# Router logits with the weights stationary in four 32-column groups, and the softmax one step later

## The reference

```
x = x + gt_m * rms_norm(mix, g_post_mix)
h = rms_norm(x, g_pre_ffn) * (1.0 + sc_f) + sh_f
aff = softmax(h @ w_router)              # 16 experts
top_v, top_i = top_k(aff.T, 2 * n // 16) # each expert picks its tokens: 32 of 256, 128 of 1024
```

## Time and profile before

| | us |
|---|---|
| median of 3 runs | 2684.17 |
| the profiled execution | 2684.22 |
| its span in the profile | 2682.4 |
| PE busy | 2538.7 (95%) |
| DVE busy | 1661.7 (62%) |
| ACT busy | 1330.4 (50%) |
| DMA moved | 345.06 MB, mean 129 GB/s |

### The profile page before, as it was taken

One profiled execution on the slowest core, in us unless ns is written; L12 is line 12 of the kernel. 1 busy time (PEld: TensorE's weight loads), 2 busy tenths in 40 slices (PEclk: granted clock), 3 DMA queues, 4 the chain that ended last, 5 costly groups with the idle time before them and its releaser, 6 DMA issues.

```text
span 2682.4 us, 37869 instructions
## 1 busy us (share of the span) xinstructions
PE 2538.7 (95%) x15199; PEld 1936.3 (72%) x15199; DVE 1661.7 (62%) x2553; ACT 1330.4 (50%) x2262; POOL 285.8 (11%) x287
## 2 busy tenths in 40 slices
PE   7999699999999999999999999996899999999994
PEld 3574499999788587676767887883677777777773
DVE  2654678886333435757576435557677767777775
ACT  3542467776423324444444333442666767666663
POOL 1441101100000001010101000000010101111012
PEclk8999899999999999999999999997899999999997
DMA  9320000000211100101002201436698898989886
GB/s 322 130 91 16 0 1 1 1 1 1 74 37 71 62 16 24 32 24 33 14 27 83 79 32 47 188 111 223 216 308 309 273 315 288 312 282 311 303 272 213
DMA packets 176608, 345.06 MB, mean 129 GB/s; under 512 B 9338, under 2 KB 37580, under 8 KB 176434
## 3 DMA queue, kind: packets, MB, share of 16 engines
q1 hardware_dynamic: 166396, 314.09, 33.0%
q0 software_dynamic: 9472, 28.32, 4.1%
q10 hardware_dynamic: 566, 0.24, 0.0%
HBM read 304.35 MB, written 38.27 MB: 128 GB/s over the span
## 4 chain that ended last, share of the span: by engine, by line
PE 62%; issue 23%; DMA 8%; DVE 4%; ACT 2%; POOL 1%; POOLq 0%; SPq 0%; DVEq 0%; ACTq 0%
PE ps L1100 16%; PE ps L1449 7%; PE ps L851 6%; DMA ffn_scratch<-WK 6%; PE ps L823 5%; PE ps L1409 5%; PE ps L228 4%; PE ps L1991 4%; PE ps L1512 2%; PE ps L1495 1%; PE ps L1423 1%; PE ps L2534 1%; PE ps L2017 1%; PE ps L1472 1%; PE ps L1393 1%
## 5 line engine op out<-in xcount | busy, mean ns | idle before, releaser
L2613 ACT ACTIVATE RWr<-R 128x1024 fp32r<-128x1024 f32 x384 | 377.7, 1054 | 72.1 <-PE ps L2534 69.4
L2708 DVE TENSOR_TENSOR W_low<-R,RWr 128x1024 fp32r<-128x1024 f32 x256 | 301.4, 1220 | 84.5 <-ACT RWr L2613 82.5
L2534 PE MATMUL ps<-RWr,R1r 128*128 128x512 f32 x1024 | 329.6, 396 | 6.0 <-DVE R1r L2696 4.2
L1100 PE MATMUL ps<-W_high,tile_high 128*128 128x512 f32 x640 | 250.9, 392 | 7.8 <-DVE W_low L1178 7.3
L1100 PE MATMUL ps<-W_low,tile_high 128*128 128x512 f32 x640 | 250.5, 391 | 0.0
L1100 PE MATMUL ps<-W_high,tile_low 128*128 128x512 f32 x640 | 250.4, 391 | 0.0
L2534 PEld LDWEIGHTS ps<-RWr,R1r 128*128 128x128 f32 x1024 | 192.9, 188 | 58.3 <-issue 14.2
L1170 DVE TENSOR_TENSOR tile_low<-R,tile_high 128x1024 fp32r<-128x1024 f32 x80 | 97.9, 1224 | 156.8 <-ACT tile_high L1126 156.6
L1449 PE MATMUL ps<-R3r 128*128 128x512 f32 (+1 forms) x640 | 188.4, 371 | 2.9 <-issue 2.9
L2708 DVE TENSOR_TENSOR tile_high<-R,RWr 128x1024 fp32r<-128x1024 f32 x128 | 150.8, 1220 | 29.9 <-ACT RWr L2613 29.6
L2534 PE MATMUL ps<-RWr,R3r 128*128 128x512 f32 x512 | 166.7, 397 | 0.0
(11 more groups left out here) (373 smaller groups left out, 5068.7 us busy)
## 6 DMA issues: line engine op xcount, KB each, us to landing
R<-in_w_dram SPq DMA_DIRECT2D x96, 2048.0 KB, 13.3
RW<-in_w_in_dram SPq DMA_DIRECT2D x11, 1024.0 KB, 5.4
R<-in_w_mod_dram SPq DMA_DIRECT2D x5, 2048.0 KB, 13.6
RW<-in_w_in_dram SPq DMA_DIRECT2D x5, 2048.0 KB, 8.3
RW<-in_w_mod_dram SPq DMA_DIRECT2D x4, 2048.0 KB, 11.7
WK<-in_w_mod_dram SPq DMA_DIRECT2D x3, 2048.0 KB, 8.0
mix_scratch<-R SPq DMA_DIRECT2D x10, 512.0 KB, 2.6
R<-mix_scratch SPq DMA_DIRECT2D x10, 512.0 KB, 6.9
```

What stands on the lines that cost most here:

```text
L1100: i = pe.matmul(bank(m % 4), Tsplit[a][:, m % 2, k, :], Wsplit[b][:, k, :], start=(k == 0 and n == 0), stop=(k == KD - 1 and n == 2))
L2534: m = pe.matmul(bank(bank_of(e, i, j)), stat[a][:, k, :], w[b][:, k % 2, :], start=(k == 0 and z == 0), stop=(k == KD - 1 and z == 2))
L2613: act.activation(ring_high[n % RING], pair_raw[i][j][:, 2 * q:2 * q + 2, :], ACT.Copy).then_inc(S("weights_high"), 1)
L2708: dve.tensor_tensor(ring_low[n % RING], pair_raw[i][j][:, 2 * q:2 * q + 2, :], ring_high[n % RING].bitcast(F32), ALU.subtract).then_inc(S( ...
```

## The change

The router's weights become the stationary operand, in groups of 32 columns (16 of weights and 16 of zeros), and the turned tile moves: product k goes to column group k % 4, two products per group, so that PSUM partitions 32c to 32c+31 hold the c-th partial sum of the logits, experts on the partitions. ACT copies the 128x128 block to SBUF (`keep_logit_sums`), and one more product with the copy stationary and the 0/1 matrix `sel_e` moving adds the four groups and turns the result in one (`logits`), into columns 128 to 143 of bank 6. The softmax reads those.

In the loops `logits(t-2)` stands behind `project(t, 1)` and ahead of `turn(t-1)`; `soft` goes from tile t-2 to tile t-3 and `turn_aff` and `keep_aff` from t-3 to t-4; `keep_logit_sums(t-2)` stands behind `soft(t-3)` on ACT. The route waits for `router_exp` of the tile before, in place of `aff_made`. The rounds of `best_eight` move from t = 5 to 8 to t = 6 to 9. The loops have NT + 4 steps.

```diff
--- before.py
+++ after.py
@@ -33,6 +33,7 @@
 NE = 16
 CAP_CTX, CAP_LAT = 2 * N_CTX // NE, 2 * N_LAT // NE
 CAP = CAP_CTX + CAP_LAT
+GROUP = 32
 EPS = 1e-6
 SCALE = float(HD) ** -0.5
 GSCALE = float(DK) ** -0.5
@@ -117,7 +118,8 @@
         st = sb("st", [P, 64])
         mhalf = sb("mhalf", [P, 16])
         w_lr = sb("w_lr", [P, KD, 2 * RANK])
-        wr = sb("wr", [P, KD * NE + P - NE])
+        wr = sb("wr", [P, KD, GROUP])
+        sel_e = sb("sel_e", [P, NE])
         with nc.sbuf_tensor("WK", [P, WORK_N], F32) as WK:
             pass
 
@@ -318,7 +320,7 @@
                 *((vv[:, 0:4, g * VW:g * VW + HD], cache_v[0, 0, g].rearrange("(b p) d -> p b d", p=P)) for g in range(HKV)),
                 (keep[:, :], k_keep),
                 (w_lr[:, :, :], win[:, C_LR:C_LR + 2 * RANK].rearrange("(k p) n -> p k n", p=P)),
-                (wr[:, 0:KD * NE].rearrange("p (k n) -> p k n", k=KD), w_router[0].rearrange("(k p) n -> p k n", p=P)),
+                (wr[:, :, 0:NE], w_router[0].rearrange("(k p) n -> p k n", p=P)),
             ):
                 sp.dma_start(dst, src, allow_slow_non_contiguous=True).then_inc(S("cache_landed"), 16)
                 n += 16
@@ -552,7 +554,7 @@
         def pool_front(pool, ch):
             pool.memset(cS4[:, :, :], 0.0).then_inc(S("cond_ready"), 1)
             ch(pool.memset(mhalf[:, :], -0.5))
-            ch(pool.memset(wr[:, KD * NE:], 0.0))
+            ch(pool.memset(wr[:, :, NE:], 0.0))
             ch(pool.memset(vv[:, :, HD::VW], 1.0))
 
             def load(t):
@@ -611,6 +613,7 @@
             ch(dve.memset(varq, 1.0))
             dve.wait_ge(S("bias_landed"), 16 * 8)
             ch(dve.tensor_reduce(sel, ident[:, :].rearrange("p (c m) -> p m c", c=4)[:, 0:2, :], AX, ALU.add))
+            ch(dve.tensor_reduce(sel_e[:, :], ident[:, :].rearrange("p (c m) -> p m c", c=4)[:, 0:NE, :], AX, ALU.add))
             dve.wait_ge(S("mod_columns"), 1)
             dve.wait_ge(S("cond_ready"), 2)
             ch(dve.tensor_copy(gv[:, :, :].rearrange("p n k -> p (n k)"), vcols[:, 56:80]))
@@ -1924,6 +1927,7 @@
 
         colb = R2[:, N_TOK:N_TOK + BLK].rearrange("p (k n) -> p k n", k=4)
         aff = R2[:, N_TOK + BLK:N_TOK + BLK + 2 * NE].rearrange("p (a n) -> p a n", a=2)
+        logit_sums = [R2[:, N_TOK + n * P:N_TOK + (n + 1) * P] for n in range(2)]
         G2b = [RW[:, j * D:(j + 1) * D] for j in range(2)]
         so = st[:, 0:24]
 
@@ -2009,13 +2013,18 @@
                 pe.wait_ge(S("h2_kept_act"), t + 1)
                 pe.wait_ge(S("h2_kept_dve"), t + 1)
                 if t >= 1:
-                    pe.wait_ge(S("aff_made"), t)
+                    pe.wait_ge(S("router_exp"), t)
                 else:
                     pe.wait_ge(S("rows_kept"), 4)
                 for k in range(KD):
 
-                    m = pe.matmul(bank(6, P), h2T[t % 2][:, k, :], wr[:, k * NE:k * NE + P], start=(k == 0), stop=(k == KD - 1))
+                    c_ = k % 4
+                    m = pe.matmul(ps[c_ * GROUP:(c_ + 1) * GROUP, 6 * BANK:6 * BANK + P], wr[:, k, :], h2T[t % 2][:, k, :], start=(k < 4), stop=(k >= 4))
                 m.then_inc(S("routed"), 1)
+
+            def logits(t):
+                pe.wait_ge(S("logit_sums_kept"), t + 1)
+                pe.matmul(ps[:, 6 * BANK + P:6 * BANK + P + NE], logit_sums[t % 2], sel_e[:, :], start=True, stop=True).then_inc(S("logits_turned"), 1)
 
             def turn_aff(t):
                 pe.wait_ge(S("aff_made"), t + 1)
@@ -2026,21 +2035,23 @@
 
             mix_turn(0)
             pe_bcast(pe, 0, 6)
-            for t in range(NT + 3):
+            for t in range(NT + 4):
                 if t < NT:
                     project(t, 0)
                 if t < 2:
                     pe_bcast(pe, 1 + 2 * t, 6)
                 if 0 <= t - 2 < NT:
                     route(t - 2)
-                if 0 <= t - 3 < NT:
-                    turn_aff(t - 3)
+                if 0 <= t - 4 < NT:
+                    turn_aff(t - 4)
                 if t + 1 < NT:
                     mix_turn(t + 1)
                 if t < NT:
                     project(t, 1)
                 if t == 0:
                     pe_bcast(pe, 2, 6)
+                if 0 <= t - 2 < NT:
+                    logits(t - 2)
                 if 0 <= t - 1 < NT:
                     turn(t - 1)
             end(pe, "pe")
@@ -2081,8 +2092,14 @@
 
             def soft(t):
                 act.wait_ge(S("router_max"), t + 1)
-                act.activation(aff[:, t % 2, :], bank(6, NE), ACT.Exp, bias=so[:, 8:9], accum_out=so[:, 9:10]).then_inc(S("router_exp"), 1)
+                act.activation(aff[:, t % 2, :], ps[:, 6 * BANK + P:6 * BANK + P + NE], ACT.Exp, bias=so[:, 8:9], accum_out=so[:, 9:10]).then_inc(S("router_exp"), 1)
                 act.wait_ge(S("router_exp"), t + 1)
+
+            def keep_logit_sums(t):
+                act.wait_ge(S("routed"), t + 1)
+                if t >= 2:
+                    act.wait_ge(S("logits_turned"), t - 1)
+                act.activation(logit_sums[t % 2], bank(6, P), ACT.Copy).then_inc(S("logit_sums_kept"), 1)
 
             def keep_aff(t):
                 act.wait_ge(S("aff_turned"), t + 1)
@@ -2097,11 +2114,13 @@
                     weights_high(cb, k)
                     if (cb, k) == (0, 1):
                         tile_high(0)
-            for t in range(NT + 3):
+            for t in range(NT + 4):
+                if 0 <= t - 3 < NT:
+                    soft(t - 3)
                 if 0 <= t - 2 < NT:
-                    soft(t - 2)
-                if 0 <= t - 3 < NT:
-                    keep_aff(t - 3)
+                    keep_logit_sums(t - 2)
+                if 0 <= t - 4 < NT:
+                    keep_aff(t - 4)
                 if t + 1 < NT:
                     tile_high(t + 1)
                 if t < NT:
@@ -2185,8 +2204,8 @@
                 dve.sem_inc(S("h2_kept_dve"), 1)
 
             def soft(t):
-                dve.wait_ge(S("routed"), t + 1)
-                ch(dve.tensor_reduce(so[:, 10:11], bank(6, NE), AX, ALU.max))
+                dve.wait_ge(S("logits_turned"), t + 1)
+                ch(dve.tensor_reduce(so[:, 10:11], ps[:, 6 * BANK + P:6 * BANK + P + NE], AX, ALU.max))
                 if t >= 2:
                     dve.wait_ge(S("aff_turned"), t - 1)
                 dve.tensor_scalar(so[:, 8:9], so[:, 10:11], -1.0, None, ALU.mult).then_inc(S("router_max"), 1)
@@ -2203,11 +2222,11 @@
                         tile_low(0)
                     if k == 3:
                         keep_row(cb)
-            for t in range(NT + 2):
+            for t in range(NT + 4):
                 if t == 1:
                     keep_row(3)
-                if 0 <= t - 2 < NT:
-                    soft(t - 2)
+                if 0 <= t - 3 < NT:
+                    soft(t - 3)
                 if t + 1 < NT:
                     tile_low(t + 1)
                 if t == 0:
@@ -2217,10 +2236,10 @@
                 if t < NT:
                     residual(t)
                     normal(t)
-                if 0 <= t - (T_CTX + 3) < CAP_CTX // 8:
+                if 0 <= t - (T_CTX + 4) < CAP_CTX // 8:
 
                     dve.wait_ge(S("aff_kept"), T_CTX)
-                    best_eight(dve, ch, 0, t - (T_CTX + 3))
+                    best_eight(dve, ch, 0, t - (T_CTX + 4))
             end(dve, "dve")
```

## The result

The changed kernel takes 2735.07 us (median of 4 runs, 2732.46 to 2737.3) against 2684.34 us for the kernel before beside it: 1.0185 times as long, 95% interval 1.0172 to 1.0197, so 50.7 us slower. Forecast were 2727.9 us, or 43.7 us slower, with a range of 2711.5 to 2745.5. The profiled execution took 2737.3 us, the longest of the four; its span is 2735.5.

A forecast was written before the change was run, and what follows sets the result against it. PE was taken as the bound, with a new closed loop through the delayed softmax. Terms 23.0 + 4.4 + 15.4 - 1.4 + 2.3 = +43.7 us on 2684.22 gave 2727.9 us, range 2711.5 to 2745.5.

The forecast's parts named there:

- The wait as the mechanism: PE's route, steps 3 to 9: it waits for the delayed exponential, due 10.74 us after the turn; +23.0 us over seven steps.
- The loop's length: Steady step from 0/1 product through exponential and route to the next turn: 18.22 us against 14.94, +3.28 each.
- rival 2: PE's route: the column groups don't run together and it stays at 1.88 us; 2745 us in all, chance 0.06.
- Entering the groups: PE, start of a burst of grouped products: costs about 0.08 us.
- Best eight: VectorE rounds behind the norm delay the exponential: 1.48 us each, three in steps 7 to 9, +4.4 us.
- The clock: PE behind each idle gap runs at a lowered clock: 2.2 us lost each, seven times, +15.4 us.
- Rival 1: PE behind the gaps: the clock holds over gaps of this length; +28.3 us, 2712.5 us in all, chance 0.10.
- rival 3: PE behind the gaps: clock never recovers before the turn, 7.2 us per gap instead of 2.2; 2763 us, chance 0.05.
- Step 2 and the tail: Step 2 routes tile 0 with a shorter route and no softmax wait, -1.4 us; the stage's last tiles, +2.3 us.
- Sum for the stage: Stage that projects the mix and routes: all terms together +43.7 us, passed through to the kernel's end.
- The memset and the load of the router's weights only change shape: nothing: Router's weights set-up: no cost, as no engine waits there.
- Rival 4: Exponential is there when PE reaches the route: 1.18 us saved in each of 8 steps; about 2677 us, chance 0.05.

The follow-up runs named there:

- the one wait alone: Kernel before, with one added wait: the route of tile t also waits for the norm of tile t+1; 2718.21 us, 1.0125 times the kernel before.
- the filled gap: Changed kernel with 17 or 23 spare 512-column products, which nobody reads, ahead of the route's wait; 2723.36 us.
- the last kernel: Changed kernel with softmax in its old step, no buffer moved, best-eight rounds behind the next mix tile's split; 2674.88 us, 0.9967 times the kernel before.
- The kernel with the buffers in place: Changed kernel with the router's weights in their old 240 words and the 0/1 matrix behind the last buffer; 2728.26 us, 1.0162 times the kernel before.

## Why the prediction was right, point by point

- The wait as the mechanism, its place and its seven times: shown. PE idles in front of the route in seven steps of the loop, released by the exponential; the one wait alone gives 38 us in the stage of the old kernel; and the same softmax with the route behind it costs next to nothing.
- The loop's length, 18.22 us: 18.15 measured with the clock held (the filled gap). In it: the turn to the exponential 10.76 for 10.74; the route 0.46 for 0.45 (1761.47 to 1761.93 in the last kernel), so the groups do run together and the bound of 1.88 is out (rival 2); the 0/1 product 0.14 for 0.25. Entering the groups costs 0.1 us in a full queue: in the last kernel the route starts 0.32 us behind the projection before it, where those stand 0.22 to 0.23 apart. That the affinities' turn changes the mode already, as the prediction says, was not tested.
- Best eight, 1.48 each on the loop: 19.63 against 18.15.
- A term that the sum lacked: the table load of ScalarE, 1.28 us in the first of the seven steps (21.68 with the half clock, 19.22 with the gap filled). The errors elsewhere in the loop hide it: 147.4 us for the seven steps forecast, 148.2 measured.
- The clock, 2.2 a gap and 15.4 in all: 15.8. The 2.2 was a choice just above the 2.1 and 1.7 of the earlier trace rows; that it came out to a tenth is in part luck, as the step with a round of best eight lost 2.8 (22.47 against 19.63). Rival 1 (the clock holds) is out, rival 3 (it stays down until the turn) too: it is back some 5 us behind the gap's end. The Trainium skill's advice against idle gaps between matmuls (TensorE: Matmul & The Clock Gate, Why this matters for your kernels) held, at 2.26 us a gap.
- Step 2 and the tail, -1.4 and +2.3: -0.9 and +2.8. In the tail it is 3.9 more in front of the last turn, for 3.7, and 1.1 less behind it, for 1.4. The last route took 0.46 us and not 0.9, as the clock was at 1.00 there again.
- Sum for the stage: 43.7 forecast, 45.1 measured in the profiled run (43.2, 2.8 and -0.9). The kernel with the buffers in place is 43.9 us slower as a whole.
- "The memset and the load of the router's weights only change shape: nothing": here the prediction failed, by 7 us. The weights' buffer grew by 16 words and got a neighbour of 16, so each buffer allocated behind it lay 128 bytes further on, and the experts' products ran 1% slower for 740 us. This is the distance between the forecast and the result: 2727.9 was forecast, and the kernel with the buffers in place took 2728.26. The stated range held it, though nothing in that range was meant for this; the prediction's own narrower range for its forecast ended at 2736.
- Rival 4 (faster) is out as a forecast, but its price was nearly right: where the route doesn't wait, the step is 13.86 us, a gain of 1.08 for the 1.18 reckoned.

## What to carry to other kernels

When a step of a software pipeline is delayed by one turn, ask of each wait that names it where its signal now falls in the waiting engine's step. Here a softmax that came 4.4 us too late for its waiter in the same step closed a loop over all engines and cost 27 us, and the idle gaps that it opened cost 16 more by the clock. And a buffer that changes size moves all behind it: keep the addresses (put the new buffer last) or measure the move alone, before a change of 1% is judged.

## What the runs showed that had not been expected

- Buffers moved by 64 or 128 bytes per partition made 738.8 us of matmuls take 746.0 to 747.6 (products 0.230 apart instead of 0.227, clock 1.00), among them products whose own operands had not moved, as those from RWr and R1r. A move of 256 bytes gave 739.0. The stages before were not longer: the first turn of the stage "out" came at 1702.40 us in the changed kernel and at 1702.15 before. Why is open.
- Four products in 32-column groups, 128 moving columns each in fp32, stand 0.029 us a record apart: 16 records in 0.46 us where the 128-column form took 1.88, 4.1 times as fast. At 1.2 GHz they took 0.83. The Trainium skill (TensorEngine Tiling (Array Packing), Theoretical Speedup) gives up to four times for a dimension of 32; the measured ratio is a little above that, and no run here shows why.
- A table load of ScalarE (1.28 us) that nobody waited for came onto PE's path when the softmax did.
- The fp32 product with 16 moving columns and a 128-column stationary adds 0.14 us for its two records in a full queue.
